# Four modulation rows of a decoder trunk summed over the partitions by GpSimd instead of TensorE

## The reference, cut to what matters

```
mod_all = jnp.einsum('bd,lde->lbe', jax.nn.silu(c), w_mod) + b_mod[:, None]
for i in range(DEPTH):
    shift1, scale1, gate1, shift2, scale2, gate2 = jnp.split(mod_all[i], N_MOD, axis=-1)
    h = rms_norm(x, norm_g[i, 0]) * (1.0 + scale1[:, None]) + shift1[:, None]
    y = pool_mixer(...) if i % 2 == 0 else diff_attention(h, ...)
    x = x + gate1[:, None] * rms_norm(y, norm_g[i, 1])
    h = rms_norm(x, norm_g[i, 2]) * (1.0 + scale2[:, None]) + shift2[:, None]
    y = swiglu(h, ...) if i % 2 == 0 else moe_swiglu(h, ...)
    x = x + gate2[:, None] * rms_norm(y, norm_g[i, 3])
```

## Time and profile before

| | |
|---|---|
| median of three runs | 1280.43 us |
| the profiled execution | 1280.07 us |
| its span (first to last instruction) | 1278.2 us |
| TensorE busy | 1249.0 us, 98% |
| VectorE busy | 387.3 us, 30% |
| ScalarE busy | 214.7 us, 17% |
| GpSimd busy | 109.8 us, 9% |
| HBM read | 465.79 MB |

### The profile page before, as it was taken

How to read it: one execution, slowest core, us unless ns; L and a number is a source line. 1 busy time by engine, 2 the same in 40 slices (tenths; PEclk the granted TensorE clock), 3 DMA queues, 4 the chain that set the end, 5 groups by cost and what they waited for, 6 DMA issues and landing times.

```text
span 1278.2 us, 31266 instructions
## 1 busy us (share of the span) xinstructions
PE 1249.0 (98%) x14625; PEld 779.1 (61%) x14625; DVE 387.3 (30%) x591; ACT 214.7 (17%) x320; POOL 109.8 (9%) x134
## 2 busy tenths in 40 slices
PE   6799999999999999999999999999999999999997
PEld 3589999989774354545455454554545545454555
DVE  1567778979872110101101011010101201011012
ACT  3253333474842000000000000000000000000001
POOL 4220000010030000020010010002001000200100
PEclk9899999999999999999999999999999999999999
DMA  9998998959379999999999999999999999999980
GB/s 371 414 358 295 334 333 305 364 197 395 123 245 420 425 423 425 424 402 424 424 407 424 424 409 411 424 409 404 423 421 396 422 424 412 404 424 415 399 355 36
DMA packets 114055, 477.47 MB, mean 374 GB/s; under 512 B 10944, under 2 KB 37280, under 8 KB 113792
## 3 DMA queue, kind: packets, MB, share of 16 engines
q1 hardware_dynamic: 106112, 457.29, 89.1%
q0 software_dynamic: 7664, 17.87, 4.6%
q10 hardware_dynamic: 144, 0.26, 0.1%
HBM read 465.79 MB, written 11.16 MB: 373 GB/s over the span
## 4 chain that ended last, share of the span: by engine, by line
PE 95%; DVE 2%; ACT 1%; POOL 1%; DMA 1%; issue 1%; SPq 0%; DVEq 0%; ACTq 0%
PE ps L2421 23%; PE ps L2407 23%; PE ps L2396 23%; PE ps L1927 7%; PE ps L1928 7%; PE ps L1929 7%; PE ps L1952 1%; PE ps L2014 1%; PE ps L1911 1%; DMA raw<-w_mod 1%; DVE wlo L1572 1%; PE ps L2205 1%; PE ps L1975 0%; PE ps L2035 0%; PE ps L2350 0%
## 5 line engine op out<-in xcount | busy, mean ns | idle before, releaser
L1799 DVE TENSOR_TENSOR act_in<-act_in,ps 128x1344 f32<-128x1344 f32 x16 | 24.9, 1555 | 527.1 <-PE ps L2407 527.1
L1927 PE MATMUL ps<-thi,whi 128*128 128x256 f32 x480 | 136.0, 283 | 0.8 <-DVE wlo L1421 0.8
L1928 PE MATMUL ps<-tlo,whi 128*128 128x256 f32 x480 | 135.8, 283 | 0.0
L1929 PE MATMUL ps<-thi,wlo 128*128 128x256 f32 x480 | 135.8, 283 | 0.0
L2396 PE MATMUL ps<-raw,turned_in 128*32 128x448 f32 x1296 | 123.7, 539 | 0.0
L2407 PE MATMUL ps<-ring_w,turned_in 128*32 128x448 f32 x1248 | 120.6, 539 | 0.0
L2421 PE MATMUL ps<-ring_w,turned_act 128*32 128x256 f32 x2016 | 117.2, 379 | 0.0
L2421 PE MATMUL ps<-raw,turned_act 128*32 128x256 f32 x2016 | 115.5, 379 | 0.0
L1220 ACT ACTIVATE act_in<-ps 128x1344 f32<-128x1344 f32 x16 | 20.7, 1292 | 548.6 <-PE ps L2396 548.6
L1290 DVE TENSOR_TENSOR wlo<-raw,whi 128x2048 fp32r<-128x2048 f32 x41 | 92.9, 2289 | 32.7 <-ACT whi L901 32.7
L2421 PEld LDWEIGHTS ps<-raw,turned_act 128*32 128x32 f32 x2016 | 82.4, 110 | 33.5 <-issue 3.5
(11 more groups left out here) (324 smaller groups left out, 1332.0 us busy)
## 6 DMA issues: line engine op xcount, KB each, us to landing
raw<-moe_w_gu SPq DMA_DIRECT2D x96, 896.0 KB, 12.9
ring_w<-moe_w_gu SPq DMA_DIRECT2D x96, 896.0 KB, 13.0
raw<-w_mod SPq DMA_DIRECT2D x84, 512.0 KB, 5.7
rows<-moe_w_gu SPq DMA_DIRECT2D x48, 896.0 KB
raw<-moe_w_down SPq DMA_DIRECT2D x48, 896.0 KB, 13.9
ring_w<-moe_w_down SPq DMA_DIRECT2D x48, 896.0 KB, 13.4
raw<-ffn_w_gu SPq DMA_DIRECT2D x44, 512.0 KB, 5.6
rows<-moe_w_down SPq DMA_DIRECT2D x24, 896.0 KB
```

Of the source, the lines that this page charges most:

```text
L1799: dve.tensor_tensor(act_3, act_3, gate_up_ps(1), ALU.mult).then_inc(e_act, 1)
L1927: pe.matmul(out, a_hi, b_hi, start=start, stop=False, skip_group_check=check)
L1928: pe.matmul(out, a_hi, b_lo, start=False, stop=False, skip_group_check=check)
L1929: return pe.matmul(out, a_lo, b_hi, start=False, stop=stop, skip_group_check=check)
```

## The change

GpSimd sums rows (1, 0), (1, 1), (0, 5) and (1, 2) over the partitions with `partition_all_reduce`, each as one instruction over 128 x 1024 numbers, issued behind the copies of the attention bias. The result is in SBUF, in `summed_rows`: three pieces of `scr`, and for the last row the place of (1, 1). A tiny multiplication on `plan` follows them on GpSimd.

VectorE turns (1, 0) and (1, 1) into columns in step 7 of the dense layer. For each block of 128 it multiplies the block by the identity and adds along the free dimension, so that partition p keeps element p: 16 instructions, each with a read of its accumulator. Row (0, 5) is finished in step 9, and (1, 2) before `project_low(0)`, with a wait for its own end, since `project_low(0)` writes over the place of the sum.

TensorE loses `row_sum(0, 5)`, both `half_sums` and `row_sum(1, 2)`. At the start of the program, the loads of the pool scale and of the first gain count one semaphore, and the first spread over the partitions waits for both.

```diff
+PE_ROWS = [(0, 2), (1, 3), (1, 4), (1, 5)]
+FINISHED_ROWS = [(0, 2), (0, 5), (1, 2), (1, 4), (1, 5)]
+POOL_ROWS = [(1, 0), (1, 1), (0, 5), (1, 2)]
+def last_mod_unit(l, g):
+    return next(r + 2 + mods.index((l, g, 3)) for _, r, _, mods, _ in FFN_STEPS if (l, g, 3) in mods)
+        summed_rows = [scr[:, 0:D], scr[:, D:2 * D], scr[:, 2 * D:3 * D], rows[:, ROW[1][1], :]]
...
             pool.wait_ge(rows_stored, 64)
+            for i, (l, g) in enumerate(POOL_ROWS):
+                pool.wait_ge(unit_done, finished(last_mod_unit(l, g)))
+                if i == 3:
+                    pool.wait_ge(row_summed, 2)
+                pool.partition_all_reduce(summed_rows[i], rows[:, ROW[l][g], :], P, bass.bass_isa.ReduceOp.add).then_inc(row_summed, 1)
+            pool.tensor_tensor(plan[:, 0:1], minus_half[:, 0:1], minus_half[:, 1:2], ALU.mult)
             next_gain(5, (0, 5))
...
-            act.wait_ge(col_ready, 6)
+            act.wait_ge(col_ready, 5)
             modulate_tile(0, 0)
-            act.wait_ge(col_ready, 8)
             modulate_tile(0, 1)
...
+                    if (l, g) in POOL_ROWS:
+                        i = POOL_ROWS.index((l, g))
+                        dve.wait_ge(row_summed, i + 1)
+                        src = summed_rows[i].rearrange("p (h d) -> p h d", h=2)
+                    else:
+                        dve.wait_ge(row_ps, row_rank(l, g))
...
+            def attention_columns():
+                for i in range(2):
+                    dve.wait_ge(row_summed, i + 1)
+                    for k in range(KC):
+                        part = summed_rows[i][:, k * P:k * P + P]
+                        ins = dve.tensor_tensor_reduce(part, part, ident, 1.0, 0.0,
+                                                       ALU.mult, ALU.add, modc[:, 1 - i, k:k + 1])
+                    ins.then_inc(col_step, 1)
+                dve.wait_ge(col_step, 4)
+                dve.scalar_tensor_tensor(modc[:, 0, :], modc[:, 0, :], 1.0, cols[:, 8, :], ALU.add, ALU.mult).then_inc(col_ready, 1)
...
                 if s == 4:
                     lambda_products()
+                if s == 7:
+                    attention_columns()
+                if s == 9:
+                    finish_rows(0, (5,))
...
-            finish_rows(0, (5,))
             low(R_QKV, Q_QKV)
...
-            attention_columns(0)
             normalize_tile(0)
             low_half(0, values_lo)
             gated_halves(1)
-            attention_columns(1)
...
+            finish_rows(1, (2,))
+            dve.wait_ge(row_done, done_rank(1, 2))
             project_low(0)
...
-            finish_rows(1, (2, 4))
+            finish_rows(1, (4,))
...
-            row_sum(0, 5)
...
-            pe.wait_ge(row_done, done_rank(0, 5))
-            half_sums(0)
             down_tile(1, last_hi, last_lo, Q_LAST_DOWN % SPL, True).then_inc(unit_used, 1)
-            half_sums(1)
...
             turn_normalized(0)
-            pe.wait_ge(col_ready, 8)
             row_sum(1, 3)
...
             pe.wait_ge(sc_max, 7)
-            row_sum(1, 2)
             turn_weights(6)
```

More of the change, by code:

```diff
@@ L122 @@
 ROW = [[0, 1, 2, 3, 4, 5], [6, 0, 1, 2, 3, 4]]
-ROW_ORDER = [[2, 5], [3, 2, 4, 5]]
+PE_ROWS = [(0, 2), (1, 3), (1, 4), (1, 5)]
+FINISHED_ROWS = [(0, 2), (0, 5), (1, 2), (1, 4), (1, 5)]
+POOL_ROWS = [(1, 0), (1, 1), (0, 5), (1, 2)]
 ROW_BANK = [[None, None, 0, None, None, 2], [None, None, 0, 2, 6, 6]]
@@ L147, in row_rank @@
 def row_rank(l, g):
-    return sum(len(order) for order in ROW_ORDER[:l]) + ROW_ORDER[l].index(g) + 1
+    return PE_ROWS.index((l, g)) + 1
 def done_rank(l, g):
-    return sum((b % 3 == 0) == (g % 3 == 0)
-               for a in range(l + 1) for b in ROW_ORDER[a] if row_rank(a, b) <= row_rank(l, g))
+    return 1 if g == 3 else FINISHED_ROWS.index((l, g)) + 1
+def last_mod_unit(l, g):
+    return next(r + 2 + mods.index((l, g, 3)) for _, r, _, mods, _ in FFN_STEPS if (l, g, 3) in mods)
 def shape_constants():
@@ L423, in build_trunk @@
         wr_loaded = sem("wr_loaded")
-        scale_loaded = sem("scale_loaded")
+        wide_loaded = sem("wide_loaded")
         gain_loaded = [sem(f"gain_loaded{i}") for i in range(2)]
         bmod_loaded = [sem(f"bmod_loaded{i}") for i in range(4)]
-        first_gain_loaded = sem("first_gain_loaded")
+        row_summed = sem("row_summed")
         wide_ps = sem("wide_ps")
@@ L722, in _ @@
             pool.dma_start(onehot, onehot_in).then_inc(small_loaded, 16)
-            pool.dma_start(wide_src[:, 0:D], pool_scale[0:1, :]).then_inc(scale_loaded, 16)
-            pool.dma_start(wide_src[:, D:2 * D], norm_g[0, 1:2, :]).then_inc(first_gain_loaded, 16)
+            pool.dma_start(wide_src[:, 0:D], pool_scale[0:1, :]).then_inc(wide_loaded, 16)
+            pool.dma_start(wide_src[:, D:2 * D], norm_g[0, 1:2, :]).then_inc(wide_loaded, 16)
             pool.memset(rows[:, 2, :], 0.0).then_inc(rows_zeroed, 1)
@@ L1325, in finish_rows @@
                 for g in groups:
-                    dve.wait_ge(row_ps, row_rank(l, g))
-                    b = ROW_BANK[l][g]
-                    src = ps[:, b:b + 2, :]
+                    if (l, g) in POOL_ROWS:
[4 more added lines that the diff above has]
+                        dve.wait_ge(row_ps, row_rank(l, g))
+                        b = ROW_BANK[l][g]
+                        src = ps[:, b:b + 2, :]
                     row = rows[:, ROW[l][g], :].rearrange("p (h d) -> p h d", h=2)
@@ L1512, in _ @@
             residual_halves(0)
-            def attention_columns(h):
-                a, b = slice(4 * h, 4 * h + 4), 3 - h
-                dve.wait_ge(col_ps, 5 + h)
-                dve.scalar_tensor_tensor(modc[:, 0, a], ps[:, b, 0:4], 1.0, cols[:, 8, a], ALU.add, ALU.mult).then_inc(col_ready, 1)
-                dve.tensor_copy(modc[:, 1, a], ps[:, b, 4:8]).then_inc(col_ready, 1)
             def low_pair(t, i):
@@ L1976, in spread @@
                 mm.then_inc(wide_ps, 1)
-            pe.wait_ge(scale_loaded, 16)
+            pe.wait_ge(wide_loaded, 32)
             spread(0, 2)
@@ L2004, in _ @@
                 mm.then_inc(pooled_ps, 1)
-            pe.wait_ge(first_gain_loaded, 16)
             spread(1, 1)
@@ L2115, in _ @@
             down_tile(0, last_hi, last_lo, Q_LAST_DOWN % SPL, True).then_inc(down_ps, 1)
-            def half_sums(h):
-                for i, g in enumerate((1, 0)):
-                    for k in range(4):
-                        mm = pe.matmul(ps[:, 3 - h, 4 * i + k:4 * i + k + 1], rows[:, ROW[1][g], (4 * h + k) * P:(4 * h + k) * P + P],
-                                       ones[:, 0:1], start=True, stop=True)
-                mm.then_inc(col_ps, 1)
             down_tile(1, ahi, alo, (q + 2) % SPL, False).then_inc(unit_used, 1)
-            pe.wait_ge(row_done, done_rank(0, 5))
-            half_sums(0)
             down_tile(1, last_hi, last_lo, Q_LAST_DOWN % SPL, True).then_inc(unit_used, 1)
-            half_sums(1)
             def turn_normalized(t):
```

## The result

The changed kernel takes **1293.59 us** (median of four runs, 1291.99 to 1295.3), the kernel before 1280.54 in the same comparison (four runs, 1277.85 to 1281.45): a ratio of 1.011, 95% interval 1.0088 to 1.0131, so 13 us or 1.0% slower. The forecast was 1281.7. The profiled execution took 1291.99 us, with a span of 1290.1.

A forecast was written before the change was run, and what follows sets the result against it. TensorE, 98% busy, was taken as the bound, with 6.8 us of removed work on its chain. Terms +2.0 - 0.05 - 1.45 + 1.2 - 0.1 + 0 = +1.6 on 1280.07 gave 1281.7 us; range 1276 to 1309.

The forecast's parts named there:

- rival A: GpSimd sums of 10 us shut out VectorE instructions with two SBUF inputs, mostly in the dense layer: 1308 us; chance 0.27.
- The sums on GpSimd: Beside the dense layer: 10 us each, done before VectorE wants them, hidden up to 11.7 us each; +0.
- Step 7: Dense layer: column products add 3.7 us on VectorE, its lead is 1.7, so TensorE's down comes +2.0 us late.
- the end of the dense layer: Removed `row_sum(0, 5)` gives -0.05 us and removed `half_sums` -1.45, as VectorE becomes the new limit.
- the start of attention: `finish_rows(1, (2,))` ahead of `project_low(0)` delays `row_max(0)`, and TensorE's `turn_weights(0)` with it: +1.2 us.
- `row_sum(1, 2)`: Its removal before `values(4)` gives only -0.1 us, since TensorE waits there for ScalarE's copy in either case.
- the wait at the third group: Sign: TensorE's third group of `down_tile` waits for VectorE's low part of the last product, until 251.7 us.
- The two rows without operands: Two GpSimd rows beside the sums with no price in the trace; taken as nothing for up to 3.4 us.
- Rival B: Sums are long (16 us) but shut nobody out; two end 8.6 us after VectorE wants them: 1290 us; chance 0.08.
- C: Rival: VectorE's leads are larger than read, so TensorE's 6.8 us come back in full: 1273.3 us; chance 0.12.

The follow-up runs named there:

- kernel without sums: Changed kernel with each GpSimd sum replaced by one clearing of its destination; no comparable time (routing changed), +1.05 us against before at the token turn.
- kernel with three rows: Paced and moved kernel with row (1,2) back on TensorE and columns between the two `low` of steps 5 and 7; 1278.69 us against 1279.73, ratio 0.9991.
- quarters in a row: Changed kernel with each sum as four instructions of 256 columns one behind the other; 1288.86 us, ratio 1.008.
- sums alone: Kernel before with the four GpSimd sums added, results unused, TensorE's sums kept; 1295.2 us against 1278.15, ratio 1.0125.
- two rows: Kernel with three rows, with row (0,5) left to TensorE too, so eight quarter sums; 1278.99 us, ratio 0.9995.
- doses: Kernel before with unused GpSimd sums of different width added in the dense layer; +8.1 us against before (one run).
- paced quarters: Changed kernel with sums in quarters of 256 columns, each released where VectorE is about to wait for ScalarE; 1287.33 us, ratio 1.0062.
- paced and moved: Paced quarters with columns split over steps 5 and 7, row (0,5) finished at its old place, (1,2) in a VectorE gap; 1282.21 us, ratio 1.0027.

## Why the forecast was wrong and its range held

The forecast was that four hidden sums and the moved work make +1.6 us. The likeliest case did not come; rival A did, at half its price. The measured time lies inside the stated range only because the range was drawn up to A's price; nothing in the forecast's own sum leads to it.

- **The sums on GpSimd** is the step that failed: "So the sums themselves are hidden up to 11.7 us each". It asks only when the results are wanted. It does not ask what VectorE can do while they run. The size was wrong on the kind side (6.1 us and not 10), and all the same 12.6 us came of it. The row that shows the mechanism was there, and I gave it 0.27 because a sum might take its inputs in pieces. It does not: a sum of 1024 columns shuts out for 4.35 us on end.
- **Step 7, the end of the dense layer, the start of attention, `row_sum(1, 2)`**: right, each within 0.4 us, but only in the kernel without sums. In the changed kernel the gap of step 7 and the wait at the third group, two of the forecast's own signs, are missing, hidden behind TensorE's larger delay. The reading that TensorE's 6.8 us on the chain would come back only where VectorE is not next holds.
- **Rival A** had place and mechanism right. Its point of decision, the length of a sum against VectorE's lead of 1.7 us, holds with two conditions: what counts is the stop and not the length of the sum, and the lead must be whole again before the next stop. The twelve quarters of the kernel with three rows, each a stop of 0.94 us, cost 0.5 us in all; quarters in a row, just as short, cost 8.70 - 1.05 = 7.65, where whole sums cost 12.6.
- **The price of rival A** was mis-sized in two ways that partly cancelled, which is luck. The stop was taken as 10 us and not as 4.35. And the deductions were too generous: for the first three sums 11.4 us of stretching became 8.54 of waiting, so only 2.9 were absorbed, for the fourth 1.14 of 3.91; together 4.0, where I took off 7.8 + 3.4. (The 2.6 for instructions that slip in between answers to 4 x 4.35 - 15.3 = 2.1.)
- **The clock** stood in no term. Of the +14.10 us at the third group the two waits are 11.3; 2.5 are the slow matmuls behind the first and 1.7 those behind the second. With the 1.72 of the removed `row_sum(0, 5)` added, 14.10 + 1.72 - 11.3 - 2.5 - 1.7 leaves 0.3.
- **The two rows without operands** got nothing for up to 3.4 us. At the first of them stands a gap of 7.0 us, most of it beside the wait for the bias copy, so that the first sum starts 2.2 us later than forecast, counted from the first down: within the bound. The one behind the last sum cost nothing in this kernel; in the paced ones it is part of what made the inverse roots late (1.5 and 2.9 us more of waiting for TensorE).
- **Rival B** (sums too long) and **C** (all 6.8 us given back) did not come: the sums were done in time, and without the stops the gain was still not there.

Left open: why the span of a sum is 1.8 us longer than the stop that it makes; what fills the gaps of 7 us and more around the sums; and what gives back the 0.41 us between `values(4)` and the token turn.

## What to carry to other kernels

Work on an idle engine isn't hidden because its result is in time: ask which instructions of other engines it stops, and compare the longest single stop with the lead of the engine that is stopped. A row in which one small instruction took ten times its usual length is worth a price in the sum. If a stop must be, cut it below the lead, release each piece where the other engine waits anyway, and let no piece run where that engine has no gap. Look also at what the helper engine has to do next: here its way back from the sums came too late for the inverse roots.

## What the runs showed of the hardware

- A `partition_all_reduce` over 128 rows takes 6.1 us for 1024 columns and 1.79 for 256, alone; the stop of VectorE is 4.35 and 0.94 us.
- Between ordinary GpSimd instructions and a sum lie 6.9 (quarters in a row) to 8.5 us (sums alone) with no instruction in the trace, and on the way back 7.0 (changed kernel) to 10.5 (two rows). The Trainium skill tells of a load of code ahead of a newly loaded GpSimd kernel, about 6 us, with no visible instruction (GPSIMD Engine Reference, section 2.1). The traces show a gap of that kind, somewhat longer, and in both directions; that it is this load is not shown. A DMA issued by GpSimd between two sums brings none: in the kernel with three rows one is issued at 141.81 and the next sum runs at 142.58.
- GpSimd instructions that read SBUF stopped VectorE instructions with two inputs from SBUF: a sum for 4.35 us, a product for 2.15, a copy for 0.85. A sum also stopped `tensor_scalar` from SBUF to SBUF (4.1 us), but nothing that took one of two inputs from PSUM; clearings stopped no instruction with two inputs.
- TensorE's waits of 8.5 us were followed by the lower clock both times, and so was that of 5.95 (quarters in a row); those of 1.0 (doses) and 1.7 us (no sums) were not. In between it varied: 2.77, 2.70 (doses) and 2.00 us (paced quarters) with it, 3.12 (paced and moved), 2.76 (sums alone) and 2.05 (paced quarters) without.
